# Two layers of a hybrid decoder trunk on one core: the shared bank read and the values scaled ahead of the softplus sums and the fold

## The chip, the cores and the metric

The kernel runs on 1 core of one Trainium2 chip, in one launch. The metric is the device time of that core in microseconds (us). The program is written engine by engine: each engine has its own list of instructions, runs it in the order written, and waits on semaphores for the others. TensorE (PE) multiplies matrices into PSUM banks; ScalarE (ACT) and VectorE (DVE) do the elementwise work; GpSimd (POOL) has little to do; SyncE (SP) issues the loads of weights.

## The reference

The sequence has 512 positions and 1024 channels, in float32. Each of two layers computes, with 8 attention heads of 64 channels, 512 channels per branch and three gates of 1024:

```python
h = rmsnorm(x, mix_norm_g)
a_b, a_c, a_x, s_u, s_v, q, k, v, gates = split(h @ w_in)
ya = short_conv(a_b, a_c, a_x, conv_w, conv_b)          # b * conv3(c * x)
yb = sgu(s_u, s_v, ln_g, ln_b, w_s, b_s)                # gelu(u) * (tril(W) ln(gelu(v)) + b)
qh, kh = rmsnorm(q per head), rmsnorm(k per head)
# stick-breaking attention, for each head and each block of 128 queries:
z = q @ k.T / 8
log_1m = where(key < query, log_sigmoid(-z), 0)
after = reverse_cumsum(log_1m) - log_1m
a = where(key < query, exp(log_sigmoid(z) + after), 0)
yc = a @ v
x = x + (sum_i sigmoid(gate_i + b_i) * (y_i @ w_branch_out[i])) @ w_o
g, u = split(rmsnorm(x) @ w_gate_up)
x = x + (silu(g) * u) @ w_down
```

## The kernel before

Everything is held transposed, channels on partitions and the 512 positions along the free axis. A weight **unit** is 1024 x 128 weights. SyncE loads it into one of four buffers `raw`; ScalarE rounds it into `w_hi` (`split_hi`, L797), VectorE takes the remainder into `w_lo` (`split_lo`, L1198), and TensorE's `unit` multiplies three products of the two halves into one of four banks (`bank`), 24 matmuls of 128x512 in all (L487, L488, L491). `scaled` (L1203) on VectorE reads a bank, multiplies it by the row norm `rstd` and frees it.

A layer first makes the first units (the gating unit's inputs, the first q and k), then runs over four **pairs** of heads, then over eight merge steps, the output projection and the feed-forward part. Three pairs are a loop on each engine (`pair(j, False, ...)`), the fourth is written out behind it (`pair(PAIRS - 1, True, ...)`). In a looped pair TensorE does, in this order: unit 1; the transposes of the pair's values (`four_transposes`, L514), read from `N0` and written to the bank `misc`; unit 2; `cumulate` for the even head (L550 to L553, running sums of the softplus into the scores' banks `z`); the column sums of q's squares (`head_squares`, L577, L578, into `misc`); unit 3; the sums of k's squares; `scores` of the odd head (L533 on); unit 4; `attend` of the even head (L567, L569, into `misc`); unit 5; `mix` of the gating unit (L595, into `misc`); unit 6; `cumulate` of the odd head; unit 7; `scores` of the next pair's even head; unit 0 of the next pair; `attend` of the odd head.

So one bank, `misc`, serves six uses in a looped pair, one after the other. TensorE waits on `misc_free` before each, and a reader frees it. For the output of `attend` the readers are `yc_half` on ScalarE (L888: copies the lower 64 partitions' part into `N1`) and then `yc_add` on VectorE (L1258: adds the other part; the semaphore is raised behind it, L1259).

The other functions that matter here, in the order of their use for one head:

- `softplus_logs` (ScalarE, L845, L848, L851): absolute value, exp and log of the scores, three instructions each, from `z` into `t_s`.
- `softplus_sum` (VectorE, L1217, three instructions): adds max(z, 0). 
- `fold_halves` (ScalarE, L861: copies the upper half of `t_s` down into `fold`), `fold_sums` (VectorE, L1229, L1231, L1233: adds the blocks' halves), `fold_round` (ScalarE, L867) and `fold_lo` (VectorE, L1242): the sums that `cumulate` multiplies for whole blocks.
- `softplus_hi` (ScalarE, L856) and `softplus_lo` (VectorE, L1222): `t_s` as a rounded part and its remainder, `cumulate`'s other input.
- `attention_exp` (ScalarE, L880 and L883, three each): exp of the accumulated scores, which also sets the banks `z` free for the next `scores`; `attention_lo` (VectorE, L1253).
- `ya_round` (ScalarE, L1015): rounds the convolution's result, which VectorE makes in `convolution` (L1452 to L1460).
- `head_square` and `square_lo` (L873, L874, L1248): the squares of q or k, in two parts; `rms_chain` and `head_norm`: their norm; `q_round`, `q_rest`, `k_round`, `k_rest`: q and k in two parts (L828, L1277, L834, L1284).

Nothing decides the order at run time: it is that of the text, engine by engine. The four stretches that the change touches are the end of a looped pair (head 1 of it, called E1 below), its middle (head 0, called E0), the same place in the last pair, and the lines ahead of the pairs' loop.

Of the kernel before, what the change touches and what calls it, by code (L numbers as in the profile page):

```python
# [68 lines left out]
M_T, M_SQ, M_SK, M_E0, M_MIX, M_E1 = range(6)  # L69
# [41 lines left out]
def build(nc, x, params, w_units, sgu_ln_g, sgu_ln_b, sgu_w, sgu_b, out):  # L111
    ctx = ExitStack()
    with ctx:
# [677 lines left out]
        def _(act):  # L791
# [49 lines left out]
            def softplus_logs(h3):  # L841

                for g, (a, n) in enumerate(S_COLS):
                    act.wait_ge(z_done, h3 + (g + 1))
                    af(t_s[:, a:a + n], z[g][:, 0:n], ACT.Abs)  # L845
                act.drain()  # L846
                for g, (a, n) in enumerate(S_COLS):
                    af(t_s[:, a:a + n], t_s[:, a:a + n], ACT.Exp, scale=-1.0)  # L848
                act.drain()
                for g, (a, n) in enumerate(S_COLS):  # L850
                    af(t_s[:, a:a + n], t_s[:, a:a + n], ACT.Ln, bias=1.0).then_inc(z_ln, 1)  # L851
# [84 lines left out]
            for l in range(L):  # L936
# [58 lines left out]
                def pair(j, last, m0):  # L995
                    at = pl["A"](j)
                    h3 = l * 24 + j * 6
                    heads = l * 8 + j * 2
                    pairs = l * PAIRS + j

                    def flat(t):
                        return t[:, bass.ds(j, 1), :].rearrange("p a t -> p (a t)")

                    def mix_slabs():

                        act.wait_ge(ln_ok, l * 4 + 4)
                        act.wait_ge(misc_done, m0 - 1)
                        for dst, src in ((mix_hi, yb_hi), (mix_lo, yb_lo)):
                            act.dma_start(dst[:, :, :].bitcast(F32),
                                          src[:, bass.ds(j, 1), :].rearrange("p a (n c) -> p (a n) c", n=NT).bitcast(F32)  # L1010
                                          ).then_inc(slab_in, 16)

                    def ya_round():
                        act.wait_ge(ya_pre, pairs + 1)
                        af(flat(ya_hi), S1[:, :], ACT.Copy).then_inc(ya_hi_ok, 1)  # L1015

                    def gelu_u():
                        act.wait_ge(u_raw, pairs + 1)
                        af(S2[:, :], S2[:, :], ACT.Gelu).then_inc(u_ok, 1)

                    def yb_round():
                        act.wait_ge(yb_pre, pairs + 1)
                        act.sem_inc(passed, 1)
                        af(flat(yb_hi), N0[:, :], ACT.Copy).then_inc(yb_hi_ok, 1)


                    split_hi(at, 3)
                    mix_slabs()
                    split_hi(at, 4)
                    act.wait_ge(misc_done, m0 + M_T + 1)  # L1030
                    af(v_both[:, :, 0, :], misc[:, :].rearrange("p (n c) -> p n c", c=HD), ACT.Copy).then_inc(v_hi_ok, 1)
                    if last:
                        split_hi(at, 5)
                        attention_exp(h3)
                        split_hi(at, 6)

                        act.wait_ge(a_lo, h3 + 3)
                        softplus_logs(h3 + 3)
                        fold_halves(h3 + 3)
                        yc_half(m0 + M_LAST_E0)  # L1040
                        softplus_hi(h3 + 3)
                        yc_round(heads, j, 0)
                        split_hi(at, 7)
                        ya_round()
                        fold_round(heads + 1)

                        gelu_u()
                        split_hi(at, 8)
                        yb_round()
                        ln_exp_table()  # L1050
                        return
                    nch = l * CHAINS + (j * 2 + 3)
                    head_square(heads + 3, QT)
                    split_hi(at, 5)

                    attention_exp(h3)
                    act.wait_ge(misc_done, m0 + M_SQ + 1)
                    head_square(heads + 4, KT)
                    rms_chain(nch, misc, HD, misc_free)
                    split_hi(at, 6)  # L1060

                    act.wait_ge(qk_nrm, heads + 3)
                    act.wait_ge(misc_done, m0 + M_SK + 1)
                    rms_chain(nch + 1, misc, HD, misc_free)
                    act.wait_ge(a_lo, h3 + 3)
                    softplus_logs(h3 + 3)
                    fold_halves(h3 + 3)

                    act.wait_ge(qk_nrm, heads + 4)
                    yc_half(m0 + M_E0)  # L1070
                    softplus_hi(h3 + 3)
                    yc_round(heads, j, 0)
                    split_hi(at, 7)
                    fold_round(heads + 1)
                    q_round()
                    split_hi(at, 8)

                    k_round()
                    ya_round()
                    split_hi(at, 9)  # L1080

                    attention_exp(h3 + 3)
                    gelu_u()
                    split_hi(at, 10)
                    yb_round()
                    ln_exp_table()

                    act.wait_ge(a_lo, h3 + 6)
                    softplus_logs(h3 + 6)
                    fold_halves(h3 + 6)  # L1090
                    yc_half(m0 + M_E1)
                    softplus_hi(h3 + 6)
                    yc_round(heads + 1, j, 1)
                    fold_round(heads + 2)
# [96 lines left out]
        def _(dve):  # L1191
# [162 lines left out]
            for l in range(L):  # L1354
# [81 lines left out]
                def pair(j, last, m0):  # L1436
# [43 lines left out]
                    if last:  # L1480
# [9 lines left out]
                        convolution()  # L1490

                        softplus_sum(h3 + 3)
                        fold_sums(heads + 1)
                        yc_add(heads, 0)
                        softplus_lo(h3 + 3)
                        yc_rest(heads, j, 0)
                        scaled(at, 4, S2[:, :])
# [31 lines left out]
                    head_norm(nch + 1, KT, par[:, R_GK:R_GK + 1])  # L1529

                    softplus_sum(h3 + 3)
                    fold_sums(heads + 1)
                    scaled(at, 4, S1[:, :])
                    yc_add(heads, 0)
                    softplus_lo(h3 + 3)
                    yc_rest(heads, j, 0)
                    split_lo(at, 7)
# [17 lines left out]
                    split_lo(at, 10)  # L1555
                    yb_rest()

                    softplus_sum(h3 + 6)
                    fold_sums(heads + 2)
                    scaled(pl["A"](j + 1), 0, N0[:, :])  # L1560
                    dve.drain()
                    dve.sem_inc(v_raw, 1)
                    yc_add(heads + 1, 1)
                    softplus_lo(h3 + 6)
                    yc_rest(heads + 1, j, 1)

# [10 lines left out]
                    dve.wait_ge(u_ok, pairs + 1)  # L1577
                    tt(N0[:, :], N0[:, :], S2[:, :], ALU.mult).then_inc(yb_pre, 1)

                softplus_sum(l * 24)  # L1580
                fold_sums(l * 8)
                scaled(pl["A"](0), 0, N0[:, :])
                dve.drain()
                dve.sem_inc(v_raw, 1)
                softplus_lo(l * 24)
                with dve.Fori(0, PAIRS - 1) as j:
                    pair(j, False, m0 + j * M_PAIR)
# [192 lines left out]
```

## Time and profile before

| | |
|---|---|
| median of 3 runs | 1709.62 us (1706.81, 1709.62, 1710.64) |
| profiled execution | 1706.89 us, of which the span of instructions is 1705.2 us |
| TensorE busy | 1663.5 us, 98% of the span |
| VectorE busy | 973.0 us, 57% |
| ScalarE busy | 789.2 us, 46% |
| GpSimd busy | 72.9 us, 4% |
| granted clock of TensorE, mean | 0.995 |
| read from HBM | 155.26 MB, 92 GB/s over the span with what is written |

The table gives averages over the whole program. The pairs of heads of layer 0 run from about 80 to about 297 us of the span; in the page's slices of 42.6 us VectorE is busy there for seven tenths and ScalarE for six to eight, while both are at three to five tenths in the feed-forward part. A granted clock of 1.00 is TensorE's full 2.4 GHz and 0.5 is 1.2 GHz.

### The profile page before, as it was taken

To read this page: it belongs to the slowest core of one execution; us is meant where nothing else is said; L and a number is where in the kernel's file an instruction comes from. 1 tells how busy PE (TensorE), PEld (TensorE's weight loads), DVE (VectorE), ACT (ScalarE), POOL (GpSimd) and SP (SyncE) were. 2 spreads that over 40 slices of the span, in tenths; PEclk is the share of its full clock that TensorE was granted. 3 is DMA by queue.
4 is the path that set the end of the run, shared out by engine and by line. 5 is a ranking of instruction groups with operands and counts; after the bars stand their busy time and mean duration, and the time that the engine had idled before them with its cause. 6 is when DMAs were issued, how large, how long until landed. Compare 5 with 4: busy or idle time off the path is not lost.

```text
span 1705.2 us, 21977 instructions
## 1 busy us (share of the span) xinstructions
PE 1663.5 (98%) x7528; PEld 1378.7 (81%) x7528; DVE 973.0 (57%) x1260; ACT 789.2 (46%) x1115; POOL 72.9 (4%) x65
## 2 busy tenths in 40 slices
PE   8999899999999999999999999999999999999999
PEld 7787777888888888888887777778888888888887
DVE  6877777554555434434548777785445544344344
ACT  7668777433343223323456777764333532232231
POOL 1200000000030000000130000000000200000000
PEclk9999999999999999999999999999999999999999
DMA  5222222222323222222332222222223222222223
GB/s 186 88 73 86 74 74 81 87 87 97 105 99 99 92 94 98 99 99 98 111 125 87 75 86 74 71 74 96 93 94 103 99 98 99 92 93 99 99 98 124
DMA packets 49153, 162.20 MB, mean 95 GB/s; under 512 B 5712, under 2 KB 5968, under 8 KB 49104
## 3 DMA queue, kind: packets, MB, share of 16 engines
q1 hardware_dynamic: 46656, 157.34, 27.4%
q10 hardware_dynamic: 2448, 4.23, 0.7%
q8 instruction: 28, 0.46, 0.1%
q14 instruction: 21, 0.17, 0.0%
HBM read 155.26 MB, written 2.10 MB: 92 GB/s over the span
## 4 chain that ended last, share of the span: by engine, by line
PE 74%; DVE 10%; ACT 8%; DVEq 3%; issue 3%; ACTq 2%; DMA 0%; SPq 0%
PE bank L487 23%; PE bank L488 23%; PE bank L491 23%; ACTq L846 1%; ACT t_s L845 1%; DVE t_s L1217 1%; PE z L488 1%; PE z L491 1%; PE z L487 1%; DVE fold L1229 1%; ACT t_s L848 1%; ACT fold L861 1%; ACT q_twice L828 1%; DVE w_lo L1198 1%; PE z L550 1%
## 5 line engine op out<-in xcount | busy, mean ns | idle before, releaser
L487 PE MATMUL bank<-xg_hi,w_hi 128*128 128x512 f32 x1584 | 624.2, 394 | 0.0
L488 PE MATMUL bank<-xg_lo,w_hi 128*128 128x512 f32 x1584 | 619.6, 391 | 0.0
L797 ACT ACTIVATE w_hi<-raw 128x1024 fp32r<-128x1024 f32 (+1 forms) x294 | 303.0, 1034 | 458.1 <-DMA raw<-in_w_units 457.4
L491 PE MATMUL bank<-xg_hi,w_lo 128*128 128x512 f32 x1584 | 391.7, 389 | 0.0
L1198 DVE TENSOR_TENSOR w_lo<-raw,w_hi 128x1024 fp32r<-128x1024 f32 (+1 forms) x294 | 359.8, 1225 | 39.2 <-ACT w_hi L797 19.7
L487 PEld LDWEIGHTS bank<-xg_hi,w_hi 128*128 128x128 f32 x1584 | 299.4, 189 | 61.6
L488 PEld LDWEIGHTS bank<-xg_lo,w_hi 128*128 128x128 f32 x1584 | 299.3, 189 | 61.2
L491 PEld LDWEIGHTS bank<-xg_hi,w_lo 128*128 128x128 f32 x1584 | 297.3, 188 | 61.8
L1203 DVE TENSOR_TENSOR S<-bank,rstd 128x512 f32<-128x512 f32 x152 | 104.9, 690 | 261.4 <-PE bank L491 259.6
L487 PE MATMUL bank<-mid_hi,w_hi 128*128 128x512 f32 x474 | 184.6, 390 | 0.0
L488 PE MATMUL bank<-mid_lo,w_hi 128*128 128x512 f32 x474 | 184.4, 389 | 0.0
L1641 DVE TENSOR_TENSOR xT<-xT,bank 128x512 f32 (+1 forms) x63 | 43.3, 687 | 160.8 <-PE bank L491 160.7
L491 PE MATMUL bank<-mid_hi,w_lo 128*128 128x512 f32 x474 | 120.3, 389 | 0.0
L487 PEld LDWEIGHTS bank<-mid_hi,w_hi 128*128 128x128 f32 x474 | 89.0, 188 | 19.0 <-DVE mid_lo L1683 0.6
L491 PEld LDWEIGHTS bank<-mid_hi,w_lo 128*128 128x128 f32 x474 | 89.0, 188 | 18.5
L488 PEld LDWEIGHTS bank<-mid_lo,w_hi 128*128 128x128 f32 x474 | 89.0, 188 | 18.4
L1166 ACT ACTIVATE mid_hi<-N 128x512 f32 (+1 forms) x44 | 27.8, 632 | 111.7 <-DVE N L1681 111.7
L1163 ACT ACTIVATE S<-S 128x512 f32<-128x512 f32 x44 | 27.9, 633 | 67.3 <-DVEq L1675 67.3
L415 POOL TENSOR_TENSOR S<-N,N 128x512 f32<-128x512 f32 x3 | 4.8, 1594 | 1133.8 <-ACT N L821 1133.8
L1683 DVE TENSOR_TENSOR mid_lo<-N,mid_hi 128x512 f32 (+1 forms) x44 | 30.5, 692 | 39.8 <-ACT mid_hi L1166 39.8
L1115 ACT ACTIVATE S<-S,par 128x512 f32<-128x512 f32 x32 | 23.2, 724 | 54.4 <-DVEq L1597 28.3
L1217 DVE SCALAR_TENSOR_TENSOR t_s<-z,t_s 128x512 f32<-128x512 f32 (+1 forms) x48 | 25.9, 595 | 34.4 <-ACT t_s L851 34.4
(202 smaller groups left out, 1606.2 us busy)
## 6 DMA issues: line engine op xcount, KB each, us to landing
raw<-in_w_units SPq DMA_DIRECT2D x278, 512.0 KB, 3.2
raw<-in_w_units SPq DMA_DIRECT2D x20, 256.0 KB, 2.9
xT<-in_x SPq DMA_DIRECT2D x8, 256.0 KB, 6.2
mix_hi<-yb_hi ACTq DMA_DIRECT2D x8, 256.0 KB, 2.3
mix_lo<-yb_lo ACTq DMA_DIRECT2D x8, 256.0 KB, 2.4
out_x<-xT SPq DMA_DIRECT2D x7, 256.0 KB, 4.3
ln_g<-in_sgu_ln_g SPq DMA_DIRECT2D x2, 256.0 KB, 4.3
ln_b<-in_sgu_ln_b SPq DMA_DIRECT2D x2, 256.0 KB, 5.1
```

The source lines that it names most:

```text
L487: mm(dst[:, :], wh[:, k0 + k, :], his[k], start=(k % per == 0), stop=False)
L488: mm(dst[:, :], wh[:, k0 + k, :], los[k], start=False, stop=False)
L491: return mm(dsts[k // per][:, :], wl[:, k0 + k, :], his[k], start=False, stop=(k % per == per - 1))
L797: af(w_hi[at.slot(c)][:, 0:kc, :], raw[at.slot(c)][:, 0:kc, :], ACT.Copy).then_inc(hi_done, 1)
L1115: af(s[:, :], gate, ACT.Sigmoid, bias=par[:, bass.ds(m + (R_BG + bias * KD), 1)]).then_inc(g_sig, 1)
L1163: af(S0[:, :], S0[:, :], ACT.Silu).then_inc(silu_ok, 1)
L1166: af(mid_hi[:, bass.ds(f, 1), :].rearrange("p a t -> p (a t)"), N0[:, :], ACT.Copy).then_inc(mid_hi_ok, 1)
L1198: tt(w[:, 0:kc, :], r[:, 0:kc, :], h[:, 0:kc, :].bitcast(F32), ALU.subtract).then_inc(lo_done, 1)
L1203: return tt(dst, bank[at.slot(c)][:, :], rstd[:, :], ALU.mult).then_inc(bank_free[at.slot(c)], 1)
L1217: stt(t_s[:, a:a + n], z[g][:, 0:n], 0.0, t_s[:, a:a + n], ALU.max, ALU.add).then_inc(sp_ok, 1)
L1641: tt(xs, xs, bank[at.slot(c)][:, :], ALU.add).then_inc(bank_free[at.slot(c)], 1)
L1683: tt(mid_lo[:, f1, :].rearrange("p a t -> p (a t)"), N0[:, :], mid_hi[:, f1, :].rearrange("p a t -> p (a t)").bitcast(F32), ALU.subtract). ...
```

## The change

The change reorders instructions on ScalarE and VectorE, with one drain added on VectorE. No operation is added, removed or given another size; TensorE's, GpSimd's and SyncE's lists are the same. It has four parts:

1. **The shared bank.** After each head's `softplus_logs`, ScalarE runs `yc_half` ahead of `fold_halves`; VectorE runs `yc_add` ahead of `fold_sums`. This is at E0 and E1 of the looped pairs and at E0 of the last pair.
2. **The wait of E0.** The wait for k's norm, which stands ahead of `yc_half` since both use `N1`, moves with it ahead of `fold_halves`.
3. **The values.** At the end of a looped pair, VectorE's `scaled` of the next pair's values into `N0`, with its signal `v_raw`, moves ahead of `softplus_sum`; ahead of the loop it moves likewise. A drain is added ahead of it within the loop, since the instruction in front of it reads `N0`.
4. **The exponentials.** In the looped pairs, ScalarE runs the odd head's `attention_exp` ahead of `ya_round` and of unit 9's `split_hi`.

```diff
@@ -1036,8 +1036,8 @@
 
                         act.wait_ge(a_lo, h3 + 3)
                         softplus_logs(h3 + 3)
+                        yc_half(m0 + M_LAST_E0)
                         fold_halves(h3 + 3)
-                        yc_half(m0 + M_LAST_E0)
                         softplus_hi(h3 + 3)
                         yc_round(heads, j, 0)
                         split_hi(at, 7)
@@ -1064,10 +1064,9 @@
                     rms_chain(nch + 1, misc, HD, misc_free)
                     act.wait_ge(a_lo, h3 + 3)
                     softplus_logs(h3 + 3)
-                    fold_halves(h3 + 3)
-
                     act.wait_ge(qk_nrm, heads + 4)
                     yc_half(m0 + M_E0)
+                    fold_halves(h3 + 3)
                     softplus_hi(h3 + 3)
                     yc_round(heads, j, 0)
                     split_hi(at, 7)
@@ -1076,10 +1075,10 @@
                     split_hi(at, 8)
 
                     k_round()
+
+                    attention_exp(h3 + 3)
                     ya_round()
                     split_hi(at, 9)
-
-                    attention_exp(h3 + 3)
                     gelu_u()
                     split_hi(at, 10)
                     yb_round()
@@ -1087,8 +1086,8 @@
 
                     act.wait_ge(a_lo, h3 + 6)
                     softplus_logs(h3 + 6)
+                    yc_half(m0 + M_E1)
                     fold_halves(h3 + 6)
-                    yc_half(m0 + M_E1)
                     softplus_hi(h3 + 6)
                     yc_round(heads + 1, j, 1)
                     fold_round(heads + 2)
@@ -1490,8 +1489,8 @@
                         convolution()
 
                         softplus_sum(h3 + 3)
+                        yc_add(heads, 0)
                         fold_sums(heads + 1)
-                        yc_add(heads, 0)
                         softplus_lo(h3 + 3)
                         yc_rest(heads, j, 0)
                         scaled(at, 4, S2[:, :])
@@ -1529,9 +1528,9 @@
                     head_norm(nch + 1, KT, par[:, R_GK:R_GK + 1])
 
                     softplus_sum(h3 + 3)
+                    yc_add(heads, 0)
                     fold_sums(heads + 1)
                     scaled(at, 4, S1[:, :])
-                    yc_add(heads, 0)
                     softplus_lo(h3 + 3)
                     yc_rest(heads, j, 0)
                     split_lo(at, 7)
@@ -1555,12 +1554,13 @@
                     split_lo(at, 10)
                     yb_rest()
 
-                    softplus_sum(h3 + 6)
-                    fold_sums(heads + 2)
+                    dve.drain()
                     scaled(pl["A"](j + 1), 0, N0[:, :])
                     dve.drain()
                     dve.sem_inc(v_raw, 1)
+                    softplus_sum(h3 + 6)
                     yc_add(heads + 1, 1)
+                    fold_sums(heads + 2)
                     softplus_lo(h3 + 6)
                     yc_rest(heads + 1, j, 1)
 
@@ -1577,11 +1577,11 @@
                     dve.wait_ge(u_ok, pairs + 1)
                     tt(N0[:, :], N0[:, :], S2[:, :], ALU.mult).then_inc(yb_pre, 1)
 
-                softplus_sum(l * 24)
-                fold_sums(l * 8)
                 scaled(pl["A"](0), 0, N0[:, :])
                 dve.drain()
                 dve.sem_inc(v_raw, 1)
+                softplus_sum(l * 24)
+                fold_sums(l * 8)
                 softplus_lo(l * 24)
                 with dve.Fori(0, PAIRS - 1) as j:
                     pair(j, False, m0 + j * M_PAIR)
```

The first place is VectorE at the end of a looped pair (E1), from the last instruction of the gating unit to the remainder of the softplus (register operations left out here and below): before,

```order
L1468 TENSOR_TENSOR yb_lo<-N_91,yb_hi 128x512
L1217 SCALAR_TENSOR_TENSOR t_s<-z,t_s 128x512
L1217 SCALAR_TENSOR_TENSOR t_s<-z,t_s 128x512
L1217 SCALAR_TENSOR_TENSOR t_s<-z,t_s 128x256
L1229 TENSOR_TENSOR fold<-fold,t_s 64x768
L1231 TENSOR_TENSOR fold<-fold 64x128
L1233 TENSOR_TENSOR fold<-fold 64x256
L1203 TENSOR_TENSOR N_91<-bank,rstd 128x512
L1258 TENSOR_TENSOR N_92<-N_92,misc 64x512
L1222 TENSOR_TENSOR s_lo<-t_s,s_hi 128x512 x2
L1222 TENSOR_TENSOR s_lo<-t_s,s_hi 128x256
```

and now:

```order
L1467 TENSOR_TENSOR yb_lo<-N_91,yb_hi 128x512
L1202 TENSOR_TENSOR N_91<-bank,rstd 128x512
L1216 SCALAR_TENSOR_TENSOR t_s<-z,t_s 128x512
L1216 SCALAR_TENSOR_TENSOR t_s<-z,t_s 128x512
L1216 SCALAR_TENSOR_TENSOR t_s<-z,t_s 128x256
L1257 TENSOR_TENSOR N_92<-N_92,misc 64x512
L1228 TENSOR_TENSOR fold<-fold,t_s 64x768
L1230 TENSOR_TENSOR fold<-fold 64x128
L1232 TENSOR_TENSOR fold<-fold 64x256
L1221 TENSOR_TENSOR s_lo<-t_s,s_hi 128x512 x2
L1221 TENSOR_TENSOR s_lo<-t_s,s_hi 128x256
```

`N_91<-bank,rstd`, the scaling of the values, moved from behind the fold to ahead of the sums, and `N_92<-N_92,misc`, which frees the bank, from behind the fold to ahead of it (VectorE's lines have numbers one lower in the changed kernel).

The second place is ScalarE at the middle of a looped pair (E0), behind the logs: `fold<-t_s` is the copy for the fold, `N_92<-misc` the copy out of the shared bank.

```order
 L851 ACTIVATE t_s<-t_s 128x512 x2
 L851 ACTIVATE t_s<-t_s 128x256
-L861 ACTIVATE fold<-t_s 64x768
-L888 ACTIVATE N_92<-misc 64x512
+L888 ACTIVATE N_92<-misc 64x512
+L861 ACTIVATE fold<-t_s 64x768
 L856 ACTIVATE s_hi<-t_s 128x512 x2
 L856 ACTIVATE s_hi<-t_s 128x256
```

The two copies changed places; the same piece of difference stands at E1.

The third place is ScalarE further on in the same pair, between the rounding of k and the table for the Gelu: `t_s<-z` and `s_hi<-t_s` are the odd head's `attention_exp`, `ya_hi<-S_85` is `ya_round`, `w_hi_63<-raw_55` the rounding of a unit.

```order
 L834 ACTIVATE k_both<-KT 64x512 x2
+L880 ACTIVATE t_s<-z 128x512 x2
+L880 ACTIVATE t_s<-z 128x256
+L883 ACTIVATE s_hi<-t_s 128x512 x2
+L883 ACTIVATE s_hi<-t_s 128x256
 L1015 ACTIVATE ya_hi<-S_85 128x512
 L797 ACTIVATE w_hi_63<-raw_55 128x1024
-L880 ACTIVATE t_s<-z 128x512 x2
-L880 ACTIVATE t_s<-z 128x256
-L883 ACTIVATE s_hi<-t_s 128x512 x2
-L883 ACTIVATE s_hi<-t_s 128x256
 L1019 ACT_TABLE_LOAD
 L1019 ACTIVATE S_86<-S_86 128x512
```

The exponentials now stand directly behind the rounding of k, and the rounding of the convolution and of the unit behind them.

## Rows read from the trace of the kernel before

**Rows 1.** The page, busy time of each engine over the span.

```profile
PE 1663.5 (98%) x7528; PEld 1378.7 (81%) x7528; DVE 973.0 (57%) x1260; ACT 789.2 (46%) x1115; POOL 72.9 (4%) x65
```

**Rows 2.** Waits of TensorE: line, released by; us in total, times, longest.

```profile
PE misc L514 <- DVEq L1259: 14.5, 6, 2.5
PE misc L514 <- DVEq L1583: 8.1, 2, 4.1
PE z L533 <- ACT t_s L880: 7.6, 6, 1.3
PE misc L595 <- DVEq L1259: 4.3, 6, 1.0
```

**Rows 3.** Windows: busy TensorE (x instructions), granted clock, DMA share, GB/s.

```profile
146.00:154.00 8.00, 7.90 (x41) 1.00 0.30 109
207.00:215.00 8.00, 7.99 (x31) 0.81 0.23 86
```

**Rows 4.** Timeline of VectorE, end of pair 1, layer 0: start, us, operation.

```profile
200.71 1.62 DVE L1217 SCALAR_TENSOR_TENSOR t_s<-z,t_s 128x512 f32<-128x512 f32 x3 [3.95 <-ACT t_s L851]
203.36 0.95 DVE L1229 TENSOR_TENSOR fold<-fold,t_s 64x768 f32<-64x768 f32 x1 [1.03 <-ACT fold L861]
205.40 0.69 DVE L1203 TENSOR_TENSOR N<-bank,rstd 128x512 f32<-128x512 f32 x1 [0.24 <-issue]
206.23 0.68 DVE L1258 TENSOR_TENSOR N<-N,misc 64x512 f32<-64x512 f32 x1
207.04 1.63 DVE L1222 TENSOR_TENSOR s_lo<-t_s,s_hi 128x512 fp32r<-128x512 f32 x3
```

**Rows 5.** Timeline of ScalarE in the same stretch.

```profile
202.36 0.85 ACT L861 ACTIVATE fold<-t_s 64x768 f32<-64x768 f32 x1 [0.86 <-DVE t_s L1217]
203.23 0.60 ACT L888 ACTIVATE N<-misc 64x512 f32<-64x512 f32 x1
```

**Rows 6.** Timeline of TensorE in the same stretch: the transposes.

```profile
207.01 1.12 PE L514 MATMUL misc<-ident_r,N 128*128 128x128 f32 x4 [2.38 <-DVEq L1259]
```

**Rows 7.** Timeline of VectorE, start of pair 1, layer 0.

```profile
146.13 1.63 DVE L1222 TENSOR_TENSOR s_lo<-t_s,s_hi 128x512 fp32r<-128x512 f32 x3
150.64 0.68 DVE L1203 TENSOR_TENSOR QT<-bank,rstd 128x512 f32<-128x512 f32 x1
152.80 0.69 DVE L1248 TENSOR_TENSOR sq_lo<-S,sq_hi 128x512 fp32r<-128x512 f32 x1 [0.57 <-ACT sq_hi L874]
```

**Rows 8.** Timeline of TensorE, start of pair 1: the sums of q's squares.

```profile
153.69 0.46 PE L577 MATMUL misc<-sq_hi,head_ones 128*128 128x512 f32 x1
```

**Rows 9.** Timeline of VectorE, middle of pair 1 (E0).

```profile
174.24 0.67 DVE L1258 TENSOR_TENSOR N<-N,misc 64x512 f32<-64x512 f32 x1
175.04 1.63 DVE L1222 TENSOR_TENSOR s_lo<-t_s,s_hi 128x512 fp32r<-128x512 f32 x3
```

**Rows 10.** Timeline of ScalarE in the same stretch.

```profile
175.02 0.63 ACT L893 ACTIVATE yc_hi<-N 64x512 f32 x1 [1.42 <-DVE N L1258]
```

**Rows 11.** Timeline of VectorE, second half of pair 1.

```profile
179.82 1.39 DVE L1277 TENSOR_TENSOR q_lo<-QT,q_twice 64x512 fp32r<-64x512 f32 x2 [0.43 <-ACT q_twice L828]
```

**Rows 12.** Timeline of ScalarE in the same stretch.

```profile
187.40 0.63 ACT L1015 ACTIVATE ya_hi<-S 128x512 f32 x1 [5.37 <-DVE S L1460]
189.00 1.36 ACT L880 ACTIVATE t_s<-z 128x512 f32<-128x512 f32 x3
```

**Rows 13.** Timeline of VectorE ahead of layer 0's pairs.

```profile
83.42 0.69 DVE L1203 TENSOR_TENSOR N<-bank,rstd 128x512 f32<-128x512 f32 x1
84.24 1.63 DVE L1222 TENSOR_TENSOR s_lo<-t_s,s_hi 128x512 fp32r<-128x512 f32 x3
```

**Rows 14.** Timeline of VectorE, layer 0, start of the last pair.

```profile
268.93 1.29 DVE L1222 TENSOR_TENSOR s_lo<-t_s,s_hi 128x512 fp32r<-128x512 f32 x2
```

**Rows 15.** Timeline of ScalarE in the middle of layer 0's last pair.

```profile
289.56 0.84 ACT L861 ACTIVATE fold<-t_s 64x768 f32<-64x768 f32 x1 [2.08 <-DVE t_s L1217]
290.54 0.60 ACT L888 ACTIVATE N<-misc 64x512 f32<-64x512 f32 x1
```

## The prediction

> **What bounds the kernel now.** I read the page's busy times first: TensorE is busy 98% of the span [rows 1], so time can only come from its remaining waits or from its clock. The list of TensorE's waits comes next: nearly all of them lie in the pairs of heads, at four places [rows 2]. The transposes wait for the shared bank at the end of each looped pair (14.5 us over 6), the first transposes of a layer for the scaled values (8.1 over 2), the next pair's scores for the exponentials (7.6 over 6), the mixing for the shared bank (4.3 over 6): 34.5 us in all. The change touches the releaser of each.
>
> Then I ask what holds the releasers. Take pair 1 of layer 0. VectorE's timeline at the pair's end shows three sums to 202.33, a fold from 203.36, then the scaling of the values, then the add that frees the bank, to 206.91 [rows 4]; the transposes start at 207.01, after 2.38 us idle [rows 6]. The same remainder instruction starts at 146.13 and at 207.04 [rows 4, 7]: the period of a pair is 60.91 us. TensorE waited in it about 2.5 + 1.2 + 1.4 = 5.1 us, so its own work is 55.8. The reader is to see that VectorE and ScalarE have a chain of their own from one remainder to the next. I followed it through the pair: remainder, q scaled at +4.51 us, its squares, the norms of q and k, logs, sums, fold, remainder, the rests of q, the convolution, the gating unit, logs, sums, fold. In it both engines wait for each other, and scarcely for TensorE, whose results all lie there a microsecond or more earlier. That chain has the 60.91 us, and TensorE follows it. So the gain of a pair is what the change takes out of this chain, not the 5.1 us that TensorE waits.
>
> **The change, part by part.**
>
> *The end of a pair (E1).* Today the remainder stands behind fold, scaling and add. With these two ahead, it starts where the scaling starts: 207.04 - 205.40 = 1.64 us earlier [rows 4]. They cost nothing at their new places. The scaling needs unit 0 of the next pair, whose matmuls end near the start of VectorE's idle 3.95 us, in which it fits [rows 4]. The add (0.68) lies between the sums' end at 202.33 and the fold at 203.36, where VectorE idles 1.03 waiting for ScalarE's copy; ScalarE's copy out of the bank (0.60) lies in its own 0.86 us of idle ahead of that copy [rows 5]. Were these covers gone, each pair would pay 0.68 and 0.60. The bank is free at about 203.1 instead of 207.0, some 2.2 us ahead of the new remainder at 205.40. The added drain stands where VectorE idles anyway.
>
> *The middle (E0).* The remainder takes the place of the add: 175.04 - 174.24 = 0.80 us earlier [rows 9]. ScalarE no longer idles 1.42 us for the add [rows 10], so it rounds q earlier, and VectorE's 0.43 us of waiting for that goes too [rows 11]. The mixing finds the bank free. Together 1.23.
>
> *The exponentials.* ScalarE idles 5.37 us ahead of the convolution's rounding [rows 12]; the six instructions, some 2.8 us, move into this gap once TensorE has accumulated. The next scores, which waited till 190.4, then wait only for k's remainder, which I put at 0.3 us. VectorE is late for nothing of it, so this part moves TensorE and not the chain: 0 in the sum, and it must be there so that TensorE stays ahead.
>
> *Ahead of the loop.* The remainder starts about 0.8 us earlier [rows 13], and the first transposes no longer wait 4 us [rows 2].
>
> *What is late next.* The chain's period becomes 60.91 - 1.64 - 1.23 = 58.04. TensorE needs 55.8 + 0.3. The difference, about 2.0 us, has to show somewhere, and it does at the sums of q's squares: VectorE's remainder of the squares ends 7.36 us after the softplus remainder starts (153.49 - 146.13) [rows 7], and TensorE came to it at 153.69, just behind it [rows 8]. In the changed kernel TensorE starts the transposes 2.2 us ahead of the softplus remainder and arrives 2.0 us before the squares. Behind this wait stand unit 3 and everything else on TensorE; VectorE and ScalarE have the results in time.
>
> *The clock.* In pairs 0 and 2 the granted clock fell to half for a while behind the wait (0.81 over 207 to 215 us, against 1.00 over 146 to 154) [rows 3]; the period from 207.04 to 268.93 is 61.89 instead of 60.91 [rows 4, 14]. It fell at four of the eight places with waits of 2.4 us and more. I expect it gone there, and half likely at each new wait of 2.0 to 2.4.
>
> The Trainium skill (TensorE: Matmul & The Clock Gate, Part 1) says that the gate's sampling runs freely against the program, so that the number of slow matmuls changes from run to run. The trace agrees: equal waits of 2.4 us lost the clock in pair 2 and kept it in pair 1. It is a reason for the width of the range and no term of the sum.
>
> The skill also says (VectorE: DVE Perf Modes, The DRAIN you can't avoid) that behind each VectorE instruction stands a flush of its duration less 266 ns. By it the two instructions at E1 would be worth 2 x 1.1 = 2.2 us in place of 1.64, and the whole change some 3 us more. The rows disagree: 205.40 to 207.04 is two instructions, drain and semaphores included, so I keep 1.64.
>
> **The sum for layer 0.** Between the remainders at 84.24 and 268.93 [rows 13, 14] lie 184.7 us. Now: 3 x 58.04 = 174.1, less 0.7 for an instruction that the first pair lacks, 173.4: 11.3 saved, with the 0.8 ahead of it 12.1. At the last pair's transposes TensorE stood level with the remainder; now it is 2.2 ahead, which makes 14.3. From there to the layer's end TensorE waits for no one by the list [rows 2], so all of it stays. Both layers: 28.6. Off goes the chance of a half clock in pair 2, whose 1.4 us nothing absorbs, once in two layers: 27.2. From the profiled execution's 1706.9 this gives 1679.7. The median of the runs is 2.7 higher, and gives 1682.4; I take the middle, **1681.0 us**.
>
> Bounds of the sum: if the 0.43 and the 0.7 to 0.8 of E0 don't come, 6 x 1.23 = 7.4 less is gained; if each new wait costs the clock and half of it gets through, 4 more is lost: 1692. If the chain has slack that I took for work (0.5 us a pair, 3 us) and the clock holds (1.4), and the low end of the runs is met: 1674.
>
> **The rivals.**
>
> *A, TensorE's waits all vanish.* The list says 34.5 us, and the four falls of the clock some 1.4 us each: about 40, for 1667. It needs the chain of VectorE and ScalarE to have been held by TensorE. For it: each wait is released earlier. Against it: the chain's waits name one another and not TensorE.
>
> *B, only part of the chain's saving arrives.* The remainder is not alone: ScalarE's rounding of the last part, the fold's rounding and the DMA issues for the gating unit behind it must keep up. If E0 brings nothing and the falling clock takes some, 18 to 20 us remain: 1689.
>
> *C, slower.* ScalarE now stands in the copy out of the shared bank before it copies for the fold. Where the attention matmuls aren't done, all behind it stalls: fold, remainder, cumulation. The last pair shows the place: the fold's copy ran at 289.56 and the other at 290.54, as soon as TensorE was done [rows 15]; the order will cost ScalarE about 1.5 us there, hidden by some 2.5 us of slack ahead of the cumulation. In the looped pairs the matmuls are done 1.2 us before the copy. If TensorE came a whole unit (5.5 us) later, each of the eight places would lose 4.3, together 34, and the kernel would end at 1712. It decides against the change from 3.6 us lost at each place (28.6 / 8), that is TensorE 4.8 us later than I place it.
>
> *D, nothing.* The waits reappear at the squares in full, since something else sets the 60.91: 1707 to 1710.
>
> **How the numbers follow.** The sum as given 0.65, A 0.08, B 0.20, C 0.03, D 0.04. The range 1671 to 1692 holds the sum and B and reaches toward A. This kernel's runs can tell 0.2% (3.4 us) from nothing. The first three cases are faster by more: 0.93. D is the same: 0.04. C is slower: 0.03.
>
> **What the changed profile would show.** Right: the waits of L514 on the shared bank and on the values near zero, L595 and L533 under 0.4 us each; a new wait of 2.0 to 2.4 us at L577 for the squares' remainder (L1247 there), six times, about 13 us in all; remainder to remainder 58.0 us; ScalarE's gap ahead of the convolution's rounding shrunk from 5.4 to about 1.5 us. Wrong: a wait at L577 near 5 us (D), or none and a period near 56 (A); a wait of ScalarE's L888 for the attention matmuls in looped pairs (C); a period of 59 or more (B).

## The result and the profile after

| | before | changed |
|---|---|---|
| median, measured together | 1709.23 us (1706.81 to 1710.64, 4 runs) | 1678.84 us (1678.02 to 1680.60, 4 runs) |
| ratio, 95% interval | | 0.9825 [0.9808, 0.9842] |
| median, measured again (after_again) | 1709.64 us (1708.53 to 1711.63, 9 runs) | 1678.92 us (1678.53 to 1679.45, 5 runs), ratio 0.9821 [0.9807, 0.9834] |
| profiled execution, its span | 1706.89, 1705.2 us | 1679.15, 1677.4 us |

The kernel became faster by 30.4 us in the medians and by 27.7 us between the two profiled executions; forecast were 1681.0 us, which is 28.2 below this median of before, and 27.2 between profiled executions.

The page of the changed kernel, busy time of each engine, beside [rows 1]:

```profile
PE 1659.0 (99%) x7528; PEld 1377.4 (82%) x7528; DVE 971.1 (58%) x1260; ACT 788.0 (47%) x1115; POOL 72.9 (4%) x65
```

Busy time is about what it was, 4.5 us less on TensorE, which fits that its clock fell at two places of the pairs instead of four. The other 23.3 of the 27.8 us of span came out of waiting. TensorE's waits in the changed kernel (line, released by; us in total, times, longest), beside [rows 2]:

```profile
PE misc L577 <- DVE sq_lo L1247: 10.5, 6, 2.2
PE z L533 <- DVE k_both L1283: 0.5, 3, 0.2
```

The four rows of [rows 2], 34.5 us, are gone. A new one stands in their place, 10.5 us over six: the sums of q's squares wait for VectorE's remainder of the squares. VectorE's timeline, start of pair 1 and end of pair 1 of layer 0, beside [rows 7] and [rows 4]:

```profile
140.99 1.63 DVE L1221 TENSOR_TENSOR s_lo<-t_s,s_hi 128x512 fp32r<-128x512 f32 x3
147.65 0.69 DVE L1247 TENSOR_TENSOR sq_lo<-S,sq_hi 128x512 fp32r<-128x512 f32 x1 [0.57 <-ACT sq_hi L874]
...
194.34 1.62 DVE L1216 SCALAR_TENSOR_TENSOR t_s<-z,t_s 128x512 f32<-128x512 f32 x3 [3.05 <-ACT t_s L851]
195.99 0.68 DVE L1257 TENSOR_TENSOR N<-N,misc 64x512 f32<-64x512 f32 x1
196.99 0.95 DVE L1228 TENSOR_TENSOR fold<-fold,t_s 64x768 f32<-64x768 f32 x1 [0.32 <-ACT fold L861]
198.92 1.63 DVE L1221 TENSOR_TENSOR s_lo<-t_s,s_hi 128x512 fp32r<-128x512 f32 x3
```

The add that frees the bank (L1257) lies at 195.99, behind the sums and ahead of the fold, in what was idle time; the fold waits 0.32 us for ScalarE in place of 1.03. The remainder of the softplus (L1221) starts at 140.99 and at 198.92: the period is 57.93 us where it was 60.91. The remainder of the squares ends at 148.34, 7.35 us after the remainder of the softplus; its old distance was 7.36. TensorE's timeline at that place, beside [rows 8]:

```profile
148.47 0.49 PE L577 MATMUL misc<-sq_hi,head_ones 128*128 128x512 f32 x1 [1.77 <-DVE sq_lo L1247]
```

The matmul starts 0.13 us after VectorE's end, after 1.77 us idle. ScalarE's timeline ahead of the convolution's rounding in pair 1, and in the middle of the last pair, beside [rows 12] and [rows 15]:

```profile
177.99 1.46 ACT L883 ACTIVATE s_hi<-t_s 128x512 fp32r<-128x512 f32 x3
181.01 0.63 ACT L1015 ACTIVATE ya_hi<-S 128x512 f32 x1 [1.56 <-DVE S L1459]
...
276.35 0.60 ACT L888 ACTIVATE N<-misc 64x512 f32<-64x512 f32 x1 [3.07 <-PE misc L569]
276.97 0.84 ACT L861 ACTIVATE fold<-t_s 64x768 f32<-64x768 f32 x1
```

The gap of 5.37 us has become 1.56, with the exponentials ahead of it. In the last pair the copy out of the bank (L888) now stands in front and waits 3.07 us for the attention matmuls; the fold's copy follows at 276.97. The granted clock (the third figure from the right) behind the new waits, beside [rows 3]:

```profile
148.00:156.00 8.00, 7.53 (x35) 1.00 0.03 5
206.00:214.00 8.00, 7.59 (x36) 1.00 0.03 6
921.00:929.00 8.00, 7.18 (x24) 0.79 0.00 1
1037.00:1045.00 8.00, 7.09 (x24) 0.79 0.05 19
```

It held at four of six waits and fell in pairs 0 and 2 of layer 1. Behind these two falls, and in no other looped pair, ScalarE's copy out of the bank waited for the attention matmuls (E0 of pairs 0 and 2 of layer 1):

```profile
938.43 0.60 ACT L888 ACTIVATE N<-misc 64x512 f32<-64x512 f32 x1 [0.46 <-PE misc L569]
1054.53 0.59 ACT L888 ACTIVATE N<-misc 64x512 f32<-64x512 f32 x1 [0.46 <-PE misc L569]
```

That is the sign that the prediction gave for rival C, in two of twelve copies of the looped pairs. It was cheap: the periods of these two pairs are 0.23 us longer than those of the same pairs in layer 0 (57.44 for 57.21 and 58.14 for 57.91).

### The profile page after: what moved, and what is told of

The parts are those of the page before. It is cut to its first block, busy times and chain, and to the rows that moved or that the text cites. A ratio compares the mean times of both kernels' runs of the same rounds, so it can differ in the third digit from the quotient of the medians.

```text
span 1677.4 us, 21983 instructions
## 1 busy us (share of the span) xinstructions
PE 1659.0 (99%) x7528; PEld 1377.4 (82%) x7528; DVE 971.1 (58%) x1260; ACT 788.0 (47%) x1115; POOL 72.9 (4%) x65
## 4 chain that ended last, share of the span: by engine, by line
PE 78%; DVE 9%; ACT 5%; DVEq 3%; issue 2%; ACTq 1%; DMA 0%; SPq 0%
PE bank L487 24%; PE bank L491 24%; PE bank L488 24%; DVEq L1510 1%; DVE w_lo L1197 1%; PE z L488 1%; PE z L491 1%; PE z L487 1%; DVE t_s L1216 1%; ACTq L846 1%; ACT t_s L845 1%; DVE s_lo L1221 1%; ACT t_s L848 1%; DVEq L1518 1%; ACT fold L861 0%
## 5 line engine op out<-in xcount | busy, mean ns | idle before, releaser
L1165 ACT ACTIVATE mid_hi<-N 128x512 f32 (+1 forms) x44 | 27.8, 632 | 112.3 <-DVE N L1681 112.3
L1114 ACT ACTIVATE S<-S,par 128x512 f32<-128x512 f32 x32 | 23.2, 724 | 55.8 <-DVEq L1597 29.7
L1616 DVE TENSOR_TENSOR N<-bank,S 128x512 f32<-128x512 f32 x16 | 11.1, 692 | 52.4 <-PE z L491 52.4
```

The source lines that it names most:

```text
L1114: af(s[:, :], gate, ACT.Sigmoid, bias=par[:, bass.ds(m + (R_BG + bias * KD), 1)]).then_inc(g_sig, 1)
L1165: af(mid_hi[:, bass.ds(f, 1), :].rearrange("p a t -> p (a t)"), N0[:, :], ACT.Copy).then_inc(mid_hi_ok, 1)
```

## The experiments

Times are medians. Kernels measured together share the runs of the kernel before: 1710.01 us beside undo_exp, only_exp, only_values and only_bank, 1709.64 beside q_first, q_late and after_again, 1709.98 beside fill_before and fill_exp. "Period" is the distance of the softplus remainders of pairs 1 and 2 in the trace.

**One part undone: the exponentials (undo_exp).**

```diff
-                    attention_exp(h3 + 3)
                     ya_round()
                     split_hi(at, 9)
+                    attention_exp(h3 + 3)
```

> The changed kernel with one part undone: ScalarE runs the odd head's exponentials behind the rounding of the convolution and of unit 9 again, as in the kernel before. Theory 1 (the period of a pair is set by the chain of VectorE and ScalarE, and TensorE only follows): the scores wait for the exponentials again, about 1.3 us in each looped pair, but the wait at the sums of q's squares (L577) shrinks by as much in pairs 1 and 2 (from 2.0 to about 1.0 us), and the remainders of the softplus keep their period of 57.9 us. Only the last of the three waits of a layer, ahead of the last pair, stays: 1.1 us for each layer, some 2 us in all over the changed kernel, about 1681. Rival (each wait of TensorE costs its length): 6 x 1.3 = 7.6 us more, 1686 to 1687.

Measured: 1680.08 us (1679.36 to 1681.10), ratio to before 0.9829 [0.9816, 0.9842]; the changed kernel's medians, measured apart from it, are 1678.84 and 1678.92. TensorE's waits:

```profile
PE misc L577 <- DVE sq_lo L1247: 6.9, 6, 2.2
PE z L533 <- ACT t_s L880: 5.2, 4, 1.3
```

The scores wait again, up to 1.3 us, and the squares wait for 6.9 us where it was 10.5: what TensorE loses at the one place it doesn't lose at the next. The period stays 57.95. The cost is 1.2 us where the sum of the waits said 7.6. The chain set the period. Forecast was 1.1 us a layer. From a layer's first transposes to its last lie 175.8 us in both layers of undo_exp; in the changed kernel it is 174.4 in layer 0 and 175.9 in layer 1. So layer 0 shows the cost, 1.4 us. Layer 1 doesn't, since only the changed kernel has a fall of the clock in pair 2 there, worth about as much.

**The exponentials alone (only_exp).** The same three lines, moved in the kernel before.

> The kernel before with the exponentials alone moved ahead of the convolution's rounding. Theory 1 (chain): the wait of the scores (L533, 7.6 us over 6) vanishes, and the wait of the transposes for the shared bank (L514) grows by the same 1.3 us each, from 14.5 to about 22 us; the time stays within 2 us of before (longer waits at one place can cost the clock more often: up to 1.4 us each, at six places). Rival (each wait counts): 7.6 us less, 1701 to 1702.

Measured: 1715.52 us (1714.87 to 1715.93), ratio 1.0035 [1.0023, 1.0047]: slower by 5.5 us, where the theory allowed 2 us either way and the rival said 7.6 less. The waits, then the windows behind three of the transposes, then ScalarE's even-head exponentials in pair 1:

```profile
PE misc L514 <- DVEq L1259: 21.6, 6, 3.7
PE misc L514 <- DVEq L1583: 8.2, 2, 4.1
```

```profile
147.00:155.00 8.00, 7.86 (x30) 0.79 0.18 66
209.00:217.00 8.00, 7.73 (x30) 0.79 0.18 66
271.00:279.00 8.00, 7.63 (x24) 0.60 0.17 66
```

```profile
155.55 1.53 ACT L880 ACTIVATE t_s<-z 128x512 f32<-128x512 f32 x3 [0.90 <-PE z L553]
```

The wait of the scores went (7.6 us, no row left) and came back at the transposes, which wait 21.6 us in place of 14.5: the swap that the chain foretells. But each of the six waits was now 3.5 to 3.7 us long, and the granted clock fell behind all eight waits of the transposes, where it had fallen behind four. TensorE's cumulation came so late that ScalarE waited 0.90 us for it, and the six periods were 61.9 to 62.2 us. In the kernel before, only the pairs with a fall had such periods (61.9 to 62.2); those of pair 1, without one, were 60.9.

**Is it the clock (fill_before, fill_exp).** To tell the clock from the new place, TensorE got work for the time of the wait:

```diff
                     unit(at, 1, xh, xl)
+                    pe.wait_ge(bank_free[at.slot(2)], at.round(2))
+                    for _ in range(9):              # 14 in fill_exp
+                        mm(bank[at.slot(2)][:, :], xg_hi[:, 0, 0:P], xh[0], start=True, stop=True)
                     four_transposes(m0 + M_T, ...)
```

> The kernel before, with nine more matmuls of 128x512 (2.1 us at the full clock) ahead of the transposes of each pair, into the bank of unit 2, which is free and is written anew afterwards: TensorE is busy in most of the wait that it has there anyway (2.4 to 2.5 us, 4.1 ahead of the first pair). They add work and change no result. Theory (the falls of the clock behind these waits are a cost of their own: 1.7 us of the chain's period in pair 0, 1.0 in pair 2): no fall in the pairs, every period 60.9 to 61.0, 2 x 2.7 = 5.4 us less than the profiled execution of before, 1701 to 1702, and a narrower spread of the runs. Rival (the work added costs and the clock is no matter): 1707 to 1713.

> The kernel before with the exponentials alone moved ahead (as only_exp, which measured 5.5 us over before), and fourteen more matmuls of 128x512 (3.2 us) in the wait of 3.7 us ahead of each pair's transposes. Theory (only_exp was slower since its longer waits, 3.7 us in place of 2.4, lost the clock at all eight places, and moving the exponentials costs and gives nothing in the chain): no fall, periods of 60.9, the same time as fill_before within 1 us, 1701 to 1702; only_exp's loss goes whole. Rival (the exponentials' new place costs the chain something): it stays 4 us or more above fill_before.

Measured: fill_before 1703.29 us (1701.65 to 1703.93), ratio 0.9962 [0.9949, 0.9976]; fill_exp 1702.05 us (1701.63 to 1702.25), ratio 0.9956 [0.9942, 0.9969]. The waits of the transposes in fill_before, then the waits of fill_exp:

```profile
PE misc L514 <- DVEq L1586: 4.1, 2, 2.1
PE misc L514 <- DVEq L1262: 2.4, 6, 0.5
```

```profile
PE misc L595 <- DVEq L1262: 5.1, 6, 1.0
PE misc L514 <- DVEq L1262: 2.4, 6, 0.5
PE misc L514 <- DVEq L1586: 1.8, 2, 0.9
```

No fall of the clock stands in either trace's pairs. With either place of the exponentials the period is 60.9 in pairs 1 and 2 and about 60.6 in pair 0, which lacks an instruction. So more matmuls made both kernels faster: the kernel before by 6.7 us (5.2 between profiled executions, 1706.89 to 1701.65, expected 5.4), the one with the moved exponentials by 13.5. The median of fill_before lies above the expected 1701 to 1702: its two runs with a granted clock of 1.000 took 1701.65 and 1701.81 us, the three with 0.999 took 1703.3 to 1703.9; all five of fill_exp had 1.000. The place of the exponentials is free in the chain, and only_exp's loss was the clock's.

**The values alone (only_values), the bank alone (only_bank).** Each is the change's part 3, or parts 1 and 2, in the kernel before; in only_bank VectorE's order at E1 is sums, add, fold, values, remainder.

> The kernel before with the scaling of the values alone moved ahead of the softplus sums (in the looped pairs and ahead of them), with the drain. Theory 1 (chain): the chain is 0.83 us shorter in each looped pair and 0.8 ahead of the loop, which is 3.3 us a layer; the clock no longer falls ahead of the first pair, about 1 us a layer. Sum 8 to 9 us, about 1700. TensorE's first wait (4.1 us twice) moves to the squares of q (about 2.4 us in the first pair) and the transposes of the later pairs still wait some 2 us each. Rival (each wait counts): the 8.1 us of the first wait and 0.83 at each of six transposes, 13 us, about 1696.

> The kernel before with the reading of the shared bank alone moved ahead of the fold (copy on ScalarE, add on VectorE, at E0 and E1 and in the last pair); the values are scaled behind the fold as before, the exponentials stand as before. Theory 1 (chain): the chain is 0.8 us shorter at E1 and 1.2 at E0, 2.0 a pair, 6.1 a layer, 12 us in all, about 1697, perhaps 2 less if the clock falls less. The transposes still wait, now for the values (v_raw), about 2 us each. With the part of the values alone (8 to 9) that makes some 21 us of the 28 to 30 of the whole change: the rest, 2.2 us a layer and more, is TensorE's lead over the remainder at the last pair, which needs both. Rival (parts add up to the whole): 20 us or more here.

Measured: only_values 1694.08 us (1693.41 to 1694.58), ratio 0.9909 [0.9896, 0.9922]; only_bank 1694.77 us (1693.34 to 1695.08), ratio 0.9914 [0.9901, 0.9927]. The waits of the first and of the second:

```profile
PE misc L514 <- DVEq L1259: 8.9, 6, 1.6
PE z L533 <- ACT t_s L880: 7.0, 6, 1.3
PE misc L577 <- DVE sq_lo L1248: 4.4, 2, 2.2
```

```profile
PE misc L514 <- DVEq L1561: 9.9, 6, 1.7
PE misc L514 <- DVEq L1582: 8.2, 2, 4.1
PE z L533 <- ACT t_s L880: 6.6, 6, 1.2
```

The periods are 60.0 and 58.9: 0.9 and 2.0 less, as the chain gives (0.83 and 2.0). The transposes still wait, in only_bank for the values (L1561, L1582). The totals are larger than I expected, 15.9 and 15.2 us instead of 8 to 9 and 12. The trace shows why: the later waits are under 2 us now, the clock fell once a layer instead of twice, and in only_values behind a place (L577 in pair 0) where it delays no one. I had priced only one fall. In the profiled executions only_values gained 12.3 us: per layer 0.8 ahead of the loop, 3 x 0.9, and the 1.7 and 1.0 of the two falls (by fill_before 1.3 to 1.6 in pair 0) make 6.2. The time alone doesn't decide against this run's rival, who said 13; the new wait at L577 and the fill runs do. With the exponentials at their old place the two parts together give undo_exp. Against my expectation, and as only_bank's rival had it (its own figure, 20 us or more for that part, was too high), they add up to about the whole: 31.2 us for 29.9 in the medians, 25.9 for 26.8 in profiled executions. They aren't independent for that. Both take the fall of pair 2 (1.0 to 1.2 us a layer, counted twice), and only with both does TensorE get ahead of the remainder at the last pair (0.85 us a layer in undo_exp, under 0.1 in either part); these two about cancel.

**The new wait as the next handle (q_first, q_late), and the changed kernel again.** q_late puts 1.14 us of other work ahead of q's scaling; q_first brings q's squares forward:

```diff
                     if last:
+                        fold_lo(heads)
+                        split_lo(at, 3)
...
                     scaled(at, 1, QT[:, :])
                     dve.drain()
                     dve.sem_inc(qk_raw, 1)
+                    fold_lo(heads)
                     v_rest()
                     square_lo(l * 6 + j * 2)
-                    split_lo(at, 4)
+                    split_lo(at, 3)
 
                     dve.wait_ge(k_ok, pairs + 1)
                     scaled(at, 2, KT[:, :])
                     dve.drain()
                     dve.sem_inc(qk_raw, 1)
+                    split_lo(at, 4)
                     split_lo(at, 5)
 
-                    attention_lo(h3)
                     square_lo(l * 6 + (j * 2 + 1))
+                    attention_lo(h3)
```

The two calls under `if last` stood ahead of it for all pairs. The squares of k come forward in the same edit.

> The changed kernel, and at the start of a looped pair VectorE scales q first, then does the fold's remainder, the values' remainder and the remainder of q's squares; unit 3's remainder follows, k is scaled ahead of unit 4's remainder, and the remainder of k's squares stands ahead of the attention's. Theory 1 (the chain of VectorE and ScalarE sets the pair's period, and TensorE has 1.8 us of waiting at L577): q's squares come some 2 us earlier, the chain gets shorter than TensorE's own work, and the period falls from 57.9 to 56.0 to 56.4 us. The waits at L577 (10.5 us over 6) go almost whole, and the falls of the clock with them: 10 to 12 us less than the changed kernel, 1667 to 1669. Rival 1 (the wait at L577 is bound by the freeing of the shared bank or by ScalarE's list, not by q's place on VectorE): under 4 us less. Rival 2 (k's squares or the weights' remainders become the new wait): 4 to 8 us less, with a wait at the second sums of a pair or at L491.

> The changed kernel with unit 4's remainder (1.14 us of VectorE) ahead of the scaling of q instead of behind it: no work more, only q's squares later by that. Theory 1 (chain): the period grows by 1.1, from 57.9 to 59.1 us, the wait at L577 by the same, and the whole by 6 x 1.14 = 6.8 us, about 1686; with waits of 3 us the clock may fall at each, whose 1.4 us count in full in pair 2 of each layer, up to 1689. Rival (there is slack behind, and only part of a delay of the chain arrives): 0 to 3 us more, 1679 to 1682.

> The changed kernel itself, on the same chip as the two above, as their measure. 1678 to 1681 us; if its profile is another one than the first, the waits at L577 again about 10 us over 6, and the clock falling at another number of them than two, since equal waits lost it and kept it before.

Measured: q_first 1668.51 us (1667.77 to 1668.94), ratio to before 0.9758 [0.9745, 0.9771]; q_late 1686.61 us (1685.70 to 1687.47), 0.9867 [0.9851, 0.9882]; the changed kernel 1678.92. The waits of q_late, then of q_first:

```profile
PE misc L577 <- DVE sq_lo L1247: 16.4, 6, 3.3
```

```profile
PE z L550 <- DVE fold_hl L1241: 3.5, 6, 1.2
```

VectorE's timeline of q_first at the start of pair 1, and TensorE's of the same stretch:

```profile
139.82 1.63 DVE L1221 TENSOR_TENSOR s_lo<-t_s,s_hi 128x512 fp32r<-128x512 f32 x3
142.21 0.69 DVE L1202 TENSOR_TENSOR QT<-bank,rstd 128x512 f32<-128x512 f32 x1
143.22 0.95 DVE L1241 TENSOR_TENSOR fold_hl<-fold,fold_hl 64x768 fp32r<-64x768 f32 x1 [0.32 <-issue]
145.14 0.69 DVE L1247 TENSOR_TENSOR sq_lo<-S,sq_hi 128x512 fp32r<-128x512 f32 x1 [0.25 <-issue]
```

```profile
144.22 0.50 PE L550 MATMUL z<-s_hi,neg_tri 128*128 128x512 f32 x1 [0.31 <-DVE fold_hl L1241]
145.96 0.49 PE L577 MATMUL misc<-sq_hi,head_ones 128*128 128x512 f32 x1
```

With 1.14 us in the chain, the wait grew by 5.9 us over six and the period to 59.0 to 59.3; the whole by 7.7 us, a little over 6 x 1.14 = 6.8, and by 6.6 to 6.9 between profiled executions. Nothing absorbed it. The clock fell at three of its six waits (2.9 to 3.3 us) instead of two, and held at one of 3.3. The squares end 6.01 us behind the softplus remainder (145.83 - 139.82) in place of 7.35, which is 1.3 us earlier and not the 2 expected; the waits at L577 went whole all the same, the period fell by 1.65 to 56.28 and the time by 10.4 us, within the 10 to 12 expected. How much of the 1.65 came from k's squares was not separated. Now TensorE's own work (60.91 less 5.1, 55.8 us by the prediction) all but sets the period, but for 3.5 us in six waits at the cumulation (L550), which waits for the fold's remainder that q was put ahead of. No fall of the clock is left in this trace's pairs. This version beats both kernels.

The profile of after_again has the wait at L577 at 10.5 us over 6 again, and the clock fell in the same two pairs as in the first profile of the changed kernel.

## Why the prediction held

**What bounds the kernel** was right: a chain of VectorE and ScalarE of 60.91 us, with TensorE behind it. undo_exp, q_late and q_first show it from three sides: a wait of TensorE given back costs almost nothing, 1.14 us put into the chain cost all of it, and the edit that brought q's squares forward by 1.3 us, and k's with them, took 1.65 us off each period, nearly down to TensorE's own work of some 56 us. That also refutes rival A for the change itself: its 1667 us needed one more edit. (The list has 2.39, 1.27 and 1.00 us for pair 1, where the prediction wrote 2.5, 1.2 and 1.4. That makes 4.7 us instead of 5.1, or about 5.3 if each counts from the start of the matmul ahead; the own work of 55.8 us is good to some 0.4.)

**The terms.** E1, 1.64, and E0, 1.23: the period fell by 2.98 where 2.87 was forecast. E0 alone: the remainder comes 28.10 us after the one of E1 (169.09 - 140.99) where it was 28.91, so 0.81 against 0.80. The two covers held: the fold starts 1.03 us behind the sums' end as before, with the add in between. The exponentials: 0 in the chain, shown by undo_exp and by fill_exp against fill_before; k's remainder was up to 0.2 us late, for 0.3. The new wait: forecast 2.0 to 2.4 us, six times, 13 in all; measured up to 2.2 and 10.5 in all, since the list counts from the modelled end of the matmul ahead (1.77 us where the starts lie 1.99 apart), and since in the pair after a fall TensorE comes later (0.81 us of wait in pair 1 of layer 1, where layer 0 has 1.77). The last pair: the fold's copy stood 12.59 us earlier than before at 276.97, while TensorE's transposes stood 14.17 us earlier (254.82 for 268.99), so 1.6 us were lost to the new order, for the 1.5 forecast, and nobody waited for them: rival C had the place right and the cover held. TensorE's gain at layer 0's last transposes was 14.2 for the forecast 14.3, and in layer 1 13.6. Its parts in layer 0: the remainder starts 12.1 us earlier at the last pair, as forecast (0.5 of it ahead of the loop for 0.8, or 0.7 by the second profile, and 11.6 in it for 11.3), and TensorE leads it by 2.0 for 2.2. Layer 1 has less since the clock fell there in pair 2, as the sum had allowed once in two layers; that it came exactly once is luck. From the transposes of pair 2 to those of the last pair lie 59.1 us there and 57.9 in layer 0: the fall cost TensorE 1.2 us, for the 1.4 priced.

**The size.** Between profiled executions the forecast missed by 0.5 us. In the medians it missed by 2.2, and the term at fault is the step from the one to the other: I took the middle of 1679.7 and 1682.4 as though the run above the profiled one stayed above by the same. The kernel before runs from 1706.8 to 1712.3 us over all jobs, and its profiled execution lies at the lower end; the changed kernel runs from 1678.0 to 1680.6. fill_before brings the kernel before down by 6.7 us in the medians and by 5.2 in profiled executions. The rest of the spread before goes with the clock too. Of its 29 runs in the three later sets, the 11 with a mean granted clock of 0.995 took 1706.85 to 1709.83 us, the 10 with 0.992 or 0.993 took 1710.02 to 1712.34. The profiled execution had 0.995. So the median of before most likely contained more time at half the clock than the trace that I read, and the change took that away as well. At which waits the clock fell in the other runs is not known, since only one has a profile.

**The clock's share.** Of the sum's 11.3 us in layer 0, 8.6 are the shorter periods (3 x 2.87); the other 2.7 are the falls in pairs 0 and 2, which stand in the 184.7 us. fill_before prices all four falls of the kernel before at 5 to 7 us, of the 30 of the change. The rule of the Trainium skill that sampling runs freely against the program (TensorE: Matmul & The Clock Gate, Part 1) stood for the width of the range; here two profiles of the changed kernel lost the clock at the same two places, but of its nine runs one, the longest (1680.60 us), had a granted clock of 0.995, the others 0.998 or 0.999. The page's word on varying falls fits that run and the spread of before; that free sampling is the cause is not shown here. On the flush behind each VectorE instruction (VectorE: DVE Perf Modes, The DRAIN you can't avoid) the measured 2.98 us a pair decides for the rows' 1.64 at E1: by the page's 2.2 it would have been 3.4.

## What to carry to other kernels

When the busiest engine waits, follow its releasers round one period before adding up its waits: if the others form a chain of their own, only what leaves that chain counts, and the waits will gather at the next place. An edit that only shortens a wait elsewhere can then be worth nothing, or less than nothing if the waits merge into one that is long enough to cost TensorE its clock. The new wait in the changed profile names the next edit, here worth another 10 us.

## What the runs showed of the hardware

How often waits of TensorE lost the full clock, by the kernels' profiles: in only_exp waits of 3.5 to 3.7 us at all six places and of 4.1 at both; in the kernel before 2.4 to 2.5 us at two of six and 4.1 at both; in q_late 2.9 to 3.3 us at three of four (held once, at 3.3) and 1.9 to 2.0 at neither of two; in the changed kernel 1.7 to 2.2 us at two of five, in both of its profiles; in undo_exp and only_values 2.2 us at both; in only_bank 4.1 us at both. Waits of 0.6 to 1.7 us lost it nowhere in undo_exp, only_values and only_bank. So in these kernels nearly equal waits lost the clock in one place and kept it in another; those of 3.5 us and more, twelve in all, lost it everywhere. A fall cost TensorE 1.2 us from one pair's transposes to the next in the changed kernel (59.1 against 57.9). It cost the chain 0.23 us of its period there, and 1.0 to 1.2 us in pair 2 of the kernel before. Matmuls whose result no one reads, set into the wait, made the kernel before faster by 0.38% [0.24%, 0.51%].
